# Sample experts of a two-layer PEER/MLA/Hyena step: steps of two rows with four buffer groups, where steps of four with two groups stood

## What is computed

```python
u = jnp.take(u_tab, i_i, axis=0)
a = jax.nn.gelu(jnp.einsum('td,thkd->thk', x_i, u))
return jnp.einsum('thk,thkd->td', a * g_i, jnp.take(v_tab, i_i, axis=0))
```

## Time and profile before

| | us |
|---|---|
| median of 3 runs | 5203.25 |
| lowest and highest | 5197.72, 5208.42 |
| the profiled execution, whole | 5209.0 |
| its span, first to last instruction | 5206.9 |
| PE busy (mean granted clock 0.880) | 3987.6 (77%) |
| DVE busy | 3348.8 (64%) |
| POOL busy | 1755.2 (34%) |
| ACT busy | 790.5 (15%) |
| HBM read | 1566.52 MB, 301 GB/s over the span |

### The profile page before, as it was taken

How to read it: one execution, slowest core, us unless ns; L and a number is a source line. 1 busy time by engine, 2 the same in 40 slices (tenths; PEclk the granted TensorE clock), 3 DMA queues, 4 the chain that set the end, 5 groups by cost and what they waited for, 6 DMA issues and landing times. The chain is left out here.

```text
span 5206.9 us, 38457 instructions
## 1 busy us (share of the span) xinstructions
PE 3987.6 (77%) x12034; PEld 2046.9 (39%) x12034; DVE 3348.8 (64%) x8112; ACT 790.5 (15%) x2180; POOL 1755.2 (34%) x1444
## 2 busy tenths in 40 slices
PE   8778966989788766677665797698977777777777
PEld 3565633454333333234332463345433332333332
DVE  0247887678776666665667688756866666645554
ACT  1212411110111111111111241101011111111111
POOL 0102343331233344444343224433124343334433
PEclk9888988999999888889887898899988888888888
DMA  6345754655899999999997575555579999999998
GB/s 240 130 177 193 259 216 185 258 218 213 343 387 386 366 380 378 385 378 392 386 392 305 195 260 223 199 228 209 202 281 387 361 384 366 360 375 383 386 385 324
DMA packets 221271, 1571.98 MB, mean 302 GB/s; under 512 B 26273, under 2 KB 28610, under 8 KB 31628
## 3 DMA queue, kind: packets, MB, share of 16 engines
q0 software_dynamic: 184320, 1342.26, 66.0%
q1 hardware_dynamic: 36748, 227.27, 11.4%
HBM read 1566.52 MB, written 2.92 MB: 301 GB/s over the span
## 5 line engine op out<-in xcount | busy, mean ns | idle before, releaser
L1881 POOL DMA_INDIRECT sb_gbufs<-in_peer_uv,sb_idx x768 | 961.2, 1252 | 1930.9 <-PE ps L992 998.4
L992 PE MATMUL ps<-sb_gbufs,sb_dge 128*128 128x512 f32 x1856 | 998.3, 698 | 409.8 <-ACT sb_dge L1223 409.7
L992 PE MATMUL ps<-sb_arena,sb_dge 128*128 128x512 f32 x1856 | 931.4, 659 | 331.9 <-ACT sb_dge L1223 330.4
L1664 DVE CUSTOM_DVE_ANT_0 sb_gbufs<-sb_gbufs,sb_keep 128x1024 f32<-128x1024 f32 x512 | 620.3, 1225 | 505.3 <-DMA sb_gbufs<-in_peer_uv,sb_idx 503.8
L1664 DVE CUSTOM_DVE_ANT_0 sb_arena<-sb_arena,sb_keep 128x1024 f32<-128x1024 f32 x512 | 621.5, 1228 | 478.8 <-DMA sb_arena<-in_peer_uv,sb_idx 477.6
L1881 POOL DMA_INDIRECT sb_arena<-in_peer_uv,sb_idx x512 | 589.1, 1151 | 896.1 <-PE ps L992 857.8
L992 PEld LDWEIGHTS ps<-sb_gbufs,sb_dge 128*128 128x128 f32 x1856 | 407.8, 226 | 969.0 <-issue 538.3
L992 PEld LDWEIGHTS ps<-sb_arena,sb_dge 128*128 128x128 f32 x1856 | 382.7, 212 | 845.7 <-issue 453.0
L1218 ACT ACTIVATE sb_small<-sb_small 128x4 f32<-128x4 f32 x256 | 52.6, 205 | 2491.8 <-DVE sb_small L1675 2482.7
L1687 DVE SCALAR_TENSOR_TENSOR sb_eacc<-sb_gbufs,sb_small,sb_eacc 128x1024 f32<-128x1024 f32 x299 | 398.9, 1334 | 9.9 <-DVE sb_small L1698 0.8
L1664 DVE CUSTOM_DVE_ANT_0 sb_gbufs<-sb_gbufs,sb_h2p 128x1024 f32<-128x1024 f32 x256 | 324.4, 1285 | 42.3 <-DMA sb_gbufs<-in_peer_uv,sb_idx 42.3
(11 more groups left out here) (231 smaller groups left out, 4149.3 us busy)
## 6 DMA issues: line engine op xcount, KB each, us to landing
sb_ring<-in_w_ada SPq DMA_DIRECT2D x48, 1024.0 KB
sb_ring<-in_w_wq SPq DMA_DIRECT2D x32, 1024.0 KB
sb_ring<-in_w_hy SPq DMA_DIRECT2D x24, 1024.0 KB
sb_ring<-in_w_ga SPq DMA_DIRECT2D x16, 1024.0 KB
sb_ring<-in_w_gb SPq DMA_DIRECT2D x16, 1024.0 KB
sb_ring<-in_w_oab SPq DMA_DIRECT2D x16, 1024.0 KB
sb_ring<-in_w_out SPq DMA_DIRECT2D x14, 1024.0 KB
sb_gbufs<-in_peer_uv,sb_idx POOLq DMA_INDIRECT x768
```

The lines of the kernel that those rows point to most:

```text
L992: q = pe.matmul(ps[:, c, :], dge[:, b, :], gbuf[b][:, D + c * 512:D + c * 512 + 512], start=(h == 0 and i == 0), stop=(h == HALVES - 1 and ...
L1664: dve.tensor_tensor_reduce(gbuf[b][:, 0:D], gbuf[b][:, 0:D], h2, 1.0, 0.0, ALU.mult, ALU.add, dots[:, q:q + 1]).then_inc(Z["ttr"], 1)
L1881: nc.gpsimd.indirect_dma_start(out=gbuf[b], out_offset=None, in_=I["peer_uv"], in_offset=bass.IndirectOffsetOnAxis(ap=idx[:, col:col + 1], ...
```

## The change

HALF becomes 2 and is no longer tied to NB, so the eight buffers form GROUPS = 4 groups of two; step m uses `m % GROUPS * HALF + i`, which for slot n is still buffer n % 8. A layer has 256 steps in place of 128. A `V` of the list still covers four slots, now two steps (TOKEN = 2), so `phases()` counts in `TOKENS_S` and `TOKENS` and gives the list that it gave. The semaphore counts and the waits for a group's earlier use go by GROUPS. DVE still adds the last slot of each four in layer 0. `add_experts` now comes after the first two dots of a new tile, not after four.

```diff
-HALF = NB // 2
+HALF = 2
+GROUPS = NB // HALF
+TOKEN = 4 // HALF
...
+TOKENS_S, TOKENS = STEPS_S // TOKEN, HALVES // TOKEN
...
-def by_vector(layer, t):
-
-    return 1 if layer < DEPTH - 1 and t > 1 else 0
+def by_vector(layer, m):
+
+    return 1 if layer < DEPTH - 1 and m >= HALVES and m % TOKEN == TOKEN - 1 else 0
...
-                b = m % 2 * HALF + i
+                b = m % GROUPS * HALF + i
...
+def of_tile(layer, t, who):
+
+    return [n for n in range((t - 1) * SLOTS, t * SLOTS) if SLOT["s", layer, n][2] == who]
...
-        for m in range(6, STEPS_S + 1):
+        for m in range(6, TOKENS_S + 1):
...
-                    yield
+                    if m % TOKEN == TOKEN - 1:
+                        yield
...
-                    q = (m % 2) * HALF
+                    q = (m % GROUPS) * HALF
...
-                    for i in range(HALF - by_vector(layer, t)):
-                        if m >= 2:
-                            act.wait_ge(Z["v_pe"], SLOT["s", layer, (m - 2) * HALF + i][3])
+                    for i in range(HALF - by_vector(layer, m)):
+                        if m >= GROUPS:
+                            act.wait_ge(Z["v_pe"], SLOT["s", layer, (m - GROUPS) * HALF + i][3])
...
-                    if m >= 2:
-                        dve.wait_ge(Z["diag"], SLOT["s", layer, (m - 2) * HALF + HALF - by_vector(layer, 1 + (m - 2) // HALVES) - 1][3])
+                    if m >= GROUPS:
+                        old = m - GROUPS
+                        dve.wait_ge(Z["diag"], SLOT["s", layer, old * HALF + HALF - by_vector(layer, old) - 1][3])
...
-                for m in range(STEPS_S + 1):
-                    if m < STEPS_S - 2:
-                        for n in range(m * HALF, m * HALF + HALF):
-                            gather("s", layer, n + 2 * HALF)
-                    yield
+                for m in range(STEPS_S):
+                    for n in range(m * HALF, m * HALF + HALF):
+                        if n + NB < (TILES - 1) * SLOTS:
+                            gather("s", layer, n + NB)
+                    if m % TOKEN == TOKEN - 1:
+                        yield
+                yield
```

More of the change, by code:

```diff
@@ L211, in expert_slots @@
         for m in range(STEPS_S):
-            own = HALF - by_vector(layer, 1 + m // HALVES)
+            own = HALF - by_vector(layer, m)
             for i in range(HALF):
-                b = m % 2 * HALF + i
+                b = m % GROUPS * HALF + i
                 take(("s", layer, m * HALF + i), b)
@@ L261, in phases @@
         between = [f"R{j}" for j in (2, 3, 4) for _ in range(PIECES)]
-        points, given, last = (len(GR[0].pace()) if more else 0), 0, STEPS_S - 10
+        points, given, last = (len(GR[0].pace()) if more else 0), 0, TOKENS_S - 10
         early = ADA_POINTS if more else 0
-        for m in range(6, STEPS_S + 1):
+        for m in range(6, TOKENS_S + 1):
             order.append("V")
-            if between and (m % 3 != 2 if more else m % HALVES >= 10 and m % 3 == 0):
+            if between and (m % 3 != 2 if more else m % TOKENS >= 10 and m % 3 == 0):
                 order.append(between.pop(0))
-            if m < HALVES and early:
+            if m < TOKENS and early:
                 order.append("P")
                 early -= 1
-            if m > HALVES and points:
-                upto = min(points, -(-points * (m - HALVES) // (last - HALVES)))
+            if m > TOKENS and points:
+                upto = min(points, -(-points * (m - TOKENS) // (last - TOKENS)))
                 order += ["P"] * (upto - given)
                 given = upto
-            if more and STEPS_S - 7 <= m < STEPS_S - 2:
+            if more and TOKENS_S - 7 <= m < TOKENS_S - 2:
                 order.append("R0")
@@ L986, in expert_step @@
                         pe.wait_ge(Z["acc_read"], layer * (TILES - 1) + t - 1)
-                    own = HALF - by_vector(layer, t)
+                    own = HALF - by_vector(layer, m)
                     for i in range(own):
@@ L1725, in add_experts @@
                 def add_experts(t):
-                    own = HALF - by_vector(layer, t)
-                    dve.wait_ge(Z["v_pe"], SLOT["s", layer, (t * HALVES - 1) * HALF + own - 1][3])
+                    dve.wait_ge(Z["v_pe"], SLOT["s", layer, of_tile(layer, t, "v_pe")[-1]][3])
                     total = ps[:, 0:2, :].rearrange("p b n -> p (b n)")
-                    if own < HALF:
+                    if of_tile(layer, t, "acc"):
                         dve.wait_ge(Z["acc"], added[0])
@@ L1750, in expert_step @@
                     t, h = 1 + m // HALVES, m % HALVES
-                    q, own = (m % 2) * HALF, HALF - by_vector(layer, t)
+                    q, own = (m % GROUPS) * HALF, HALF - by_vector(layer, m)
                     for i in range(HALF):
@@ L1765, in expert_step @@
                         for i in range(own, HALF):
-                            add_value("s", layer, m * HALF + i, q + i, h == 0 and i == own)
+                            add_value("s", layer, m * HALF + i, q + i, m * HALF + i == of_tile(layer, t, "acc")[0])
                     if layer == DEPTH - 1 and t > 1 and h == 3:
@@ L1874, in gather @@
                         pool.wait_ge(Z["gw"], 4 * layer + tile)
-                    if n == HALF:
+                    if n == 4:
                         pool.wait_ge(S["h2"], START[2 * layer + 1]["h2"] + 4)
@@ L1897, in expert_step @@
                     return
-                for m in range(STEPS_S + 1):
-                    if m < STEPS_S - 2:
-                        for n in range(m * HALF, m * HALF + HALF):
-                            gather("s", layer, n + 2 * HALF)
-                    yield
+                for m in range(STEPS_S):
+                    for n in range(m * HALF, m * HALF + HALF):
+                        if n + NB < (TILES - 1) * SLOTS:
+                            gather("s", layer, n + NB)
+                    if m % TOKEN == TOKEN - 1:
+                        yield
+                yield
             def first_gathers(layer):
-                for n in range(2 * HALF):
+                for n in range(NB):
                     gather("s", layer, n)
```

## The result

| | before | after |
|---|---|---|
| median | 5204.86 us | 5045.85 us |
| lowest and highest | 5197.72, 5208.42 | 5037.75, 5050.47 |
| the profiled execution (its span) | 5209.0 (5206.9) | 5050.47 (5048.5) |
| mean granted clock of PE | 0.880 | 0.911 |

The medians lie 159 us apart; after / before over the runs compared is 0.9686, with a 95% interval of 0.966 to 0.9712 (the two medians alone give 0.969). In the row of lowest and highest, a single disturbed run of before, of 16744 us, is left out; without it the median of before is 5203.25. The forecast was 5015, in a range of 4930 to 5115; the time lies 31 us above the forecast, inside the range.

What follows compares the result with a forecast made beforehand. The prediction took a gather buffer's turnaround (21.1 us against 19.8 at 423 GB/s) as the limit, not the queue; its terms summed to -188, from 5209.0 to 5021, hence 5015 us at the median, range 4930 to 5115.

Steps and rivals of the forecast that it cites:

- 1, slots 32-127: Layer 0, 1370 to 1681 us, full of routing pieces on DVE: half of the 21 us above 423 GB/s comes, -10.
- 2, slots 128-479: Layer 0, 1681 to 2753 us, dense work between turns: 70% of the 104 us above 423 GB/s comes, -73.
- 3, last 32 slots: Layer 0, 2753 to 2847 us: queue needs 74 us, DVE 89; with a little waiting 90, so -4.
- 4, routing in layer 1: Layer 1, 3848 to 4488 us, fifteen routing pieces: 60% of the 73 us above 423 GB/s comes, -44.
- 5, the plain loop: Layer 1, 4488 to 5187 us, almost only the loop: 85% of the 74 us above 423 GB/s comes, -63.
- 6, the starts: Start of each layer's expert block: DVE sets the pace, 8 added passages of 0.83 us each, +13.
- 7, the ends: Behind the last dot PE has two slots left, not four: 3.6 us less, twice, -7.
- The signs named ahead: Profile after: experts at 400 GB/s or more, even gather waits, 3.6 us PE bursts, layer 1 clock over 0.95.
- Rival A: Sample's expert stretches: the 423 GB/s ceiling is reached and all of the difference comes, 4933 us; chance 12%.
- Rival B: Gather queue gives little more, gathers just wait longer in it; only the ends change, 5203 us; chance 8%.
- Rival C: Layer 0: dense weights' loads come late beside a fuller gather queue and hold PE; slower, 5315 us; chance 10%.
- Rival D: Pauses of 1.4 us bring PE's clock to 1.2 GHz and keep it there; about 5800 us; chance 2%.

Runs made afterwards that it cites:

- Short_add: The changed kernel, but DVE adds its own slots of the sample over 8 of 1024 columns, leaving out part of the sum; 5035.22 us, ratio 0.9666.
- all_on_pe: The changed kernel with all slots of layer 0 added on PE, none by DVE; 5048.65 us, ratio 0.9698.
- small_twice: The changed kernel with four more small chained DVE instructions per pair, on a spare buffer; 5087.69 us, ratio 0.9771.
- fours_pe_filled: The kernel before with two extra unused matmuls on PE per step of layer 1 from step 8 on, after the third gather lands; 5150.27 us, ratio 0.9898.

## Why the prediction came out as it did

The mechanism was right: the turn of a buffer set the pace, pairs brought it under the queue's 19.8 us, and the queue sets the pace now. The size was overstated, 188 us against 158 in the profiled executions (5206.9 - 5048.5). Term by term, from the first two rows of the table above:

| step | expected | measured | why |
|---|---|---|---|
| 1, slots 32-127 | -10 | -6 | 394 to 401 GB/s |
| 2, slots 128-479 | -73 | -54 | 382 to 403 GB/s, 52% of the difference and not 70% |
| 3, last 32 slots | -4 | +2 | DVE busy 87 of 97 us |
| 4, routing in layer 1 | -44 | -42 | 375 to 402 GB/s, 58% |
| 5, the plain loop | -63 | -56 | 378 to 409 GB/s, 76% |
| 6, the starts | +13 | +3 | hidden by DVE's idle time |
| 7, the ends | -7 | -6 | 3.5 us behind the last slot, 2.9 in the middle |

- **Step 2 is the term that was mis-sized**, with 19 of the 30 us. Its share of 70% was chosen for the dense pieces and rested on no row. Short_add, all_on_pe and small_twice show that it is neither DVE's nor PE's load. The crossed waits of four dense pieces account for 8 to 12 us of the 49 that remain above 968. Some 37 to 41 us stay open: each other placement of the pieces that was tried cost more than it gave. They are not spread evenly: in the kernel after slots 160 to 191 ran at 422 GB/s, slots 128 to 159 just before them at 369.
- **Step 3** named the bound rightly, but took almost no waiting on top of DVE's 89 us; 10 us of it came. Here DVE's load counts: with less of it the 32 slots take 92.1 (short_add) and 90.7 us (all_on_pe), with more 104.5 (small_twice).
- **Step 6** priced eight passages of 0.83 us per start as if all lay on the path. DVE had 26 us idle in a start of 151, and its busy time rose by 4.5 us. Small_twice adds about 12 us of DVE's work to each start and lengthens them by 1 to 2 us.
- **Steps 4 and 5** came near with both chosen shares, and fours_pe_filled tells them apart: 52 of 56 us in the plain loop are PE's clock, 17 of 42 beside routing. The prediction held the clock for one part of the turn's 2.55 + 9.43; it gave no split, and whether layer 0 divides in the same way was not tested; the clock of slots 128 to 479 rose only from 0.85 to 0.88. The turn of 21.1 us, taken from one chain, was low as well: 699 us for 256 slots are 21.8 per eight.
- **The signs named ahead.** The rate of 400 and more came in all stretches but the last 32 slots and the starts, DVE's waits in layer 1 lost their gap, bursts of 8 took 3.70 us with pauses of 1.26, and the granted clock is 0.98 in the plain loop, though 0.92 and not over 0.95 beside routing. The chain has more DMA and less PE (13% and 10%, from 11% and 14%). Wrong was "mean matmul near 450 ns": the page's mean still holds the overlap of one matmul with the next and stands at 620 and 608 ns there, while from start to start it is 3.71 / 8 = 464 ns. The small instructions kept their length, here those that make dw, 165 ns on two columns where L1761 took 167 on four:

```profile
L1771 DVE SCALAR_TENSOR_TENSOR sb_small<-sb_small 128x2 f32<-128x2 f32 x512 | 84.5, 165 | 103.0 <-ACT sb_small L1227 96.4
```

- **Rival A** (4933, all of the difference) is nearest in the plain loop, 643 against 625. The turn has room there: for 500 us on end the rate is 421, and 32 slots take 80.5 us, against 79.3 at 423 GB/s. The rest is at the two ends of the stretch, the first 31 us, behind a tile's end, at 286 GB/s, and the last 12, where the queue runs out, at 152.
- **Rival B** had half a truth in it: the gathers do wait longer in the queue, 13.36 us from issue to landing. They do so at a higher rate, 421 against 385.
- **Rival C** fell: PE's waits for w_gb and w_oab in layer 0 went from 7.9 and 7.4 us to 7.4 and 8.8 us.
- **Rival D** fell: pauses of 1.26 us leave the clock at 0.98, and the rule of the Trainium skill named there (TensorE: Matmul & The Clock Gate, "A second HAM failure mode: psum-queue depth-cycling") is not borne out by pauses of this length. Its other side was the main effect: the long pauses of the kernel before were what cost the clock.

## What to carry to other kernels

Where a loop gathers through a ring of buffers, set the turn of one buffer (issue to landing, compute, next issue) against the time that the queue needs for all of them, and compare the moved GB/s with the best short stretch, not with the DMA share. If the turn is the longer, smaller steps help twice, by a shorter hold and by shorter pauses on PE, which then keeps its clock; below the queue's time a still smaller step only adds work. The spare time of a turn is what carries the loop over other work: two buffers fewer cost 214 us here. An order in which PE is put ahead by one turn should be looked through for pieces whose first input another engine makes behind that same turn.

## What the runs showed of the hardware

- The queue of indirect gathers held 420 to 422 GB/s for four slices on end, 505 us, with 128 rows of 8 KB per transfer, picked by the tokens' indices. Twenty us of the kernel after, in the columns of the earlier trace rows:

```profile
4470.00:4490.00 20.00, 14.93 (x34) 5.77 (x33) 12.25 (x32) 3.59 (x12) 7.49 (x8) 1.00 1.01 422
```

  That is nearly the 423 of the earlier trace rows, now for long. The 358 GB/s for one core that the prediction took from the Trainium skill (DMA: Bandwidth & Descriptors, "Where 436 GB/s comes from") does not bound this kernel. The Trainium skill (HBM Reference, "Specifications (TRN2)") puts a core that streams alone at about 425 GB/s, and the trace, at 422, agrees.
- A DMA share of 0.95 stood beside 375 GB/s, one of 0.98 beside 403 and one of 1.01 beside 422: the share nears its end before the rate does.
- The small DVE instruction that makes dw took 165 ns on two columns and 167 on four; those added in small_twice took 180 ns. A passage is thus paid by the number of its instructions: 38 us of DVE for 64 passages of four are 0.60 each.
- PE's busy time for the same instructions fell from 521 to 477 us in the plain loop when its pauses went from 4.7 to 1.3 us and the mean clock from 0.86 to 0.98. The clock is not all that sets it: with single slots it is 506 us at a clock of 0.99.
